# First attention: scaling-and-transposing products on two row halves, 64 queries each, into two banks

## The reference, cut to what matters

```
s = einsum("bqhpd,bkhpd->bhpqk", q, k) * (HEAD_DIM ** -0.5)
p = softmax(s, axis=-1)
a = p[:, :, 0] - lam * p[:, :, 1]
o = einsum("bhqk,bkhe->bqhe", a, v)
```

## Time and profile before

| | |
|---|---|
| median of three runs | 1553.6 us (1548.66 to 1557.16) |
| profiled execution | 1554.42 us |
| its span | 1552.6 us, mean granted TensorE clock 0.988 |
| TensorE multiplying, loading | busy 96%, 89% |
| VectorE, ScalarE | busy 73%, 49% |
| first attention's loops on TensorE | 169.6 to 246.5 us |
| transposing records (L969) | 256, busy 34.4 us |

### The profile page before, as it was taken

The page is one execution under the profiler, slowest core; times in us unless marked ns, Lnnn a source line. Parts: engine busy times, 40 slices in busy tenths (PEclk is TensorE's granted clock), DMA queues, the critical chain, the costliest instruction groups (busy, mean ns, idle before and its releaser), DMA issues.

```text
span 1552.6 us, 27950 instructions
## 1 busy us (share of the span) xinstructions
PE 1495.9 (96%) x11704; PEld 1384.9 (89%) x11704; DVE 1132.0 (73%) x1572; ACT 765.0 (49%) x911; POOL 11.5 (1%) x25
## 2 busy tenths in 40 slices
PE   7999999999999999999999999999999999999887
PEld 3999778999998886899999999988999999998786
DVE  6877785878887977655667566676587666878886
ACT  2422354566334441566434446544454334668784
POOL 0000000000000000000001000000000000000000
PEclk9999999999999999999999999999999999999999
DMA  9454434477775430245666454322354455778993
GB/s 370 154 204 148 152 111 165 149 281 271 292 279 214 178 136 27 109 175 194 227 236 245 167 186 160 141 104 110 140 199 159 164 195 190 299 291 323 361 370 117
DMA packets 43525, 310.27 MB, mean 200 GB/s; under 512 B 5239, under 2 KB 5624, under 8 KB 7000
## 3 DMA queue, kind: packets, MB, share of 16 engines
q1 hardware_dynamic: 41760, 301.75, 52.1%
q0 software_dynamic: 1264, 5.82, 1.1%
q10 hardware_dynamic: 392, 1.12, 0.2%
HBM read 307.63 MB, written 1.05 MB: 199 GB/s over the span
## 4 chain that ended last, share of the span: by engine, by line
PE 82%; DVE 9%; DMA 4%; ACT 3%; issue 1%; SPq 0%; DVEq 0%; ACTq 0%
PE ps L754 16%; PE ps L755 15%; PE ps L759 15%; DVE wlo L2240 3%; PE ps L969 2%; DMA raw<-weights_in 2%; PE ps L790 2%; PE ps L785 2%; PE ps L786 2%; ACT whi L1687 2%; PE ps L807 1%; DMA mstart<-mod_start_in 1%; PE ps L808 1%; PE ps L809 1%; PE ps L727 1%; PE ps L729 1%
## 5 line engine op out<-in xcount | busy, mean ns | idle before, releaser
L2240 DVE TENSOR_TENSOR wlo<-raw,whi 128x2048 fp32r<-128x2048 f32 x172 | 392.6, 2288 | 167.6 <-ACT whi L1687 166.8
L1687 ACT ACTIVATE whi<-raw 128x2048 fp32r<-128x2048 f32 x187 | 357.3, 1915 | 202.1 <-PE ps L759 114.7
L754 PE MATMUL ps<-uhi,whi 128*128 128x256 f32 x1232 | 294.4, 281 | 0.8 <-DVE y L2865 0.8
L755 PE MATMUL ps<-uhi,wlo 128*128 128x256 f32 x1232 | 288.4, 277 | 0.0
L754 PEld LDWEIGHTS ps<-uhi,whi 128*128 128x128 f32 x1232 | 231.4, 188 | 7.7 <-issue 6.3
L755 PEld LDWEIGHTS ps<-uhi,wlo 128*128 128x128 f32 x1232 | 231.3, 188 | 1.3 <-issue 1.2
L759 PE MATMUL ps<-ulo,whi 128*128 128x256 f32 x1232 | 164.9, 276 | 0.0
L759 PEld LDWEIGHTS ps<-ulo,whi 128*128 128x128 f32 x1232 | 151.3, 188 | 0.0
L754 PE MATMUL ps<-hid_hi,whi 128*128 128x256 f32 x512 | 122.1, 281 | 0.0
L755 PE MATMUL ps<-hid_hi,wlo 128*128 128x256 f32 x512 | 120.8, 278 | 0.0
L2259 DVE SCALAR_TENSOR_TENSOR macc<-raw,csil,macc 128x256 f32<-128x256 f32 x224 | 108.6, 485 | 7.8
(11 more groups left out here) (611 smaller groups left out, 3214.2 us busy)
## 6 DMA issues: line engine op xcount, KB each, us to landing
raw<-weights_in SPq DMA_DIRECT2D x225, 1024.0 KB, 4.8
raw_more<-weights_in SPq DMA_DIRECT2D x22, 1024.0 KB, 4.9
y<-weights_in SPq DMA_DIRECT2D x15, 1024.0 KB, 6.6
spare<-weights_in SPq DMA_DIRECT2D x14, 1024.0 KB, 6.6
mstart<-mod_start_in SPq DMA_DIRECT2D x4, 2048.0 KB, 18.8
w1c<-cmp_w_in POOLq DMA_DIRECT2D x1, 2048.0 KB, 13.6
h<-x_in SPq DMA_DIRECT2D x1, 1024.0 KB, 7.8
ctx<-ctx_in SPq DMA_DIRECT2D x1, 1024.0 KB, 30.1
```

The lines of the kernel that those rows point to most:

```text
L754: mm(o, wk(whi, k), x0[:, k0 + k, :], start=first and k == 0, stop=False)
L755: mm(o, wk(wlo, k), x0[:, k0 + k, :], start=False, stop=False)
L1687: fn(hi_at(i) if n is None else whi[:, sl, :], raw_at(i) if n is None else raw[:, sl, :], ACT.Copy).then_inc(s("hi_ready"), 1)
L2240: tt(lo_at(i), raw_at(i), f32(hi_at(i)), ALU.subtract).then_inc(s("lo_ready"), 1)
```

## The change

Each product of a block with the diagonal becomes two: the queries 0 to 63 (rows 0 to 63 of `ebuf`, the upper left quarter of `diag`) and the queries 64 to 127 (rows and columns 64 to 127). The two have 64 contraction rows each, stream 64 columns each, and write to two banks, 4 for the first half of the queries and 5 for the second. Off these quarters the diagonal matrix is zero, so nothing is lost. A unit now fills half of both banks, and the next unit uses the same places: TensorE waits for the copy of the unit just before (`att_copied` at u, not u - 1), from unit 1 on. ScalarE copies in two parts of 128x256, and it makes the copy of unit u - 2 ahead of `exps(u)`.

```
             def turn_weights(u):
                 pe.wait_ge(s("att_ready"), u + 1)
-                if u >= 2:
-                    pe.wait_ge(s("att_copied"), u - 1)
+                if u:
+                    pe.wait_ge(s("att_copied"), u)
                 for k in range(4):
                     for p in range(2):
-                        ins = mm(ps[:, 4 + u % 2, k * P:(k + 1) * P], ebuf[:, u % 2, p, k * P:(k + 1) * P], diag[:, u % 2, p, :],
-                                 start=p == 0, stop=p == 1)
+                        for half in range(2):
+                            a = slice(half * HD, (half + 1) * HD)
+                            ins = mm(ps[:, 4 + half, k * HD:(k + 1) * HD], ebuf[a, u % 2, p, k * P:(k + 1) * P], diag[a, u % 2, p, a],
+                                     start=p == 0, stop=p == 1)
                 ins.then_inc(s("att_turned"), 1)
...
             for u in range(2 * HEADS + 4):
-                if u < 2 * HEADS:
-                    exps(u)
                 if 2 <= u <= 2 * HEADS + 1:
                     v = u - 2
                     act.wait_ge(s("att_turned"), v + 1)
                     if v >= 4:
                         act.wait_ge(s("o_ready"), v // 2 - 1)
-                    fn(atb[:, (v // 2) % 2, :, (v % 2) * P:(v % 2 + 1) * P], ps[:, 4 + v % 2, :].rearrange("p (k q) -> p k q", k=4),
-                       ACT.Copy).then_inc(s("att_copied"), 1)
+                    for half in range(2):
+                        q0 = (v % 2) * P + half * HD
+                        ins = fn(atb[:, (v // 2) % 2, :, q0:q0 + HD], ps[:, 4 + half, 0:T].rearrange("p (k q) -> p k q", k=4), ACT.Copy)
+                    ins.then_inc(s("att_copied"), 1)
+                if u < 2 * HEADS:
+                    exps(u)
```

## The result

The changed kernel took 1554.62 us (12 runs, 1550.98 to 1567.6), the kernel before 1550.2 (12 runs). The ratio is 1.004, interval 1.0021 to 1.006: slower by 3 to 9 us, around the 0.5% that I had called no change for three runs, but not the +0.5 us of the sum. The mean granted clock of the changed kernel's runs is 0.9864. The profiled executions hide the difference: span 1552.5 after, 1552.6 before. The one before, 1554.42, was among the slower of its kernel (the 12 runs: 1544.98 to 1557.16). So the base of the sum, 1553.6, stood 3.4 us above the 1550.2, the move was put 4 us too low against the medians, and the predicted 1554.1 met the 1554.62 by luck of that base.

The account below looks back on a forecast made before the run. TensorE's own sequence was taken to bound the kernel, 82% of the last chain. Products 0, switches -0.6 and -0.3, end +1.4 gave +0.5 us: 1554.9 against the profiled execution, 1554.1 against the median, range 1548 to 1561.

Parts of the forecast that it names:

- the sum: Whole kernel: products 0, switches -0.6 and -0.3, end +1.4, together +0.5 us on the profiled 1554.42.
- Products: Turning units on TensorE: 128-column loads set the step, halves load together, 16 pairs at 0.112, 1.79 us; no change.
- A: Rival, turning units: the stream sets the step, each unit 0.86 us less, 13.8 in all, 1540.3; chance 4%.
- B: Rival, turning units: halves do not load wide weights together, +1.79 us a unit, +28.6, 1582.7; chance 4%.
- Switches: Row-mode changes around TensorE's units: -0.05 us each for units 2 to 13, -0.6, and -0.3 at the start.
- -0.3 of the first two units: Row-mode changes at the start, half clock: unit 1 loses 0.28 and 0.2 us, unit 0 gains 0.2.
- The wait: TensorE waiting for the previous unit's copy: hidden except between units 14 and 15, where it idles 1.09 us.
- +1.4: Attention's end, units 14 and 15: 1.09 us of idle TensorE plus 0.35 for row-mode changes.
- ScalarE's later exponentials: ScalarE copying first moves exponentials back by some 0.6 us; no cost taken, 1 us if a copy slips.
- C: Rival, turns with modulation: the copy comes late, 0.86 us on 7 units, +6, 1560; chance 3%.
- The clock: TensorE's granted clock in the first attention: expected at 1.00 from 185 us on, no cost in the sum.
- rival D: First attention: half-filled products keep the granted clock low, pieces at most double, +57 us, 1611; chance 2%.

Follow-up runs that it names:

- 128 columns streamed: Changed kernel with each half product streaming all 128 diagonal columns, 64 of them zero, instead of 64; ratio 1.0012 to the kernel before, 1551.49 us.
- quarters: Changed kernel with each half product cut again by keys, weights 64 columns wide, 64 records a unit; ratio 0.9979 to the kernel before, 1546.51 us.
- 128 columns and head squares: Changed kernel streaming all 128 diagonal columns, with the first six head-square sums moved between units 14 and 15; ratio 1.0004 to the kernel before, 1551.18 us.
- idle products ahead: Changed kernel with extra unused TensorE products, two behind the second scores and three behind the third; ratio 1.0029 to the kernel before, 1553.96 us.
- head squares between: Changed kernel with the first six head-square sums moved from behind unit 15 to between units 14 and 15; ratio 1.0028 to the kernel before, 1553.08 us.
- at the start with idle products: Kernel before with only extra unused TensorE products added, two behind the second scores and three behind the third; ratio 0.9994, 1550.34 us.

## Why the prediction was right or wrong

**Products, right.** The step is set by the load of 128 columns and both halves load at once: 16 pairs a unit, 1.73 in the chain. Halving the stream saved nothing (128 columns streamed: 1.78), halving the weights' columns did (quarters: 1.16). Rivals A and B fall. The 0.071 of L1253, a mean over two orders, could not decide this; the units do. The Trainium skill's rule in "TensorE: Matmul & The Clock Gate", LDWEIGHTS (a load goes by its columns, not by its rows), agrees with these three numbers in their order, though 1.16 is more than half of 1.73; the up to 2x of its "TensorEngine Tiling (Array Packing)", Theoretical Speedup, came for the quarters, which narrow the weights' columns as well, in part (1.16 against 1.73), and for the halves not at all.

**Switches, right.** 0.11 us per pair of turns, 0.05 a unit, came back, as summed. The -0.3 of the first two units cannot be read off, since they ran at another clock.

**The wait, right in place and size.** One idle stretch, ended by the copy. The wait alone cost +1.0 in the profile of the kernel before; in that of the kernel with 128 columns, from unit 14's start to the values behind the head squares, it is 7.58 us (233.82 to 241.40) against 6.25 before (234.38 to 240.63), +1.3 with the switches, where I had put +1.4. ScalarE's later exponentials held nobody up; C did not come.

**The clock, wrong.** The step that failed is rival D, in what I set against it: "records follow without gaps as before". They do, loads and all, and the clock still fell. I had given D 2%, and only at the price of the whole attention at 1.2 GHz, which did not come either; a part of it did. All my other chances, 98%, had gone to a clock that stays. The size: over the runs the clock is 0.9863 against 0.9903, and 0.0040 of some 1550 us is 6.2 us of TensorE at full speed; the means of those runs are 1556.59 and 1550.70, 5.9 apart. Among the 35 runs of the kernel before in that comparison 0.001 of clock goes with 1.3 us, and by this rate the 0.0040 is 5.4. For the kernel before with 64 columns it is 0.0057, 8.8 us or 7.6 by that rate, against 7.3 between the means. So most of the loss is the clock, with the wait's 1.0 beside it, within the noise of twelve runs (0.001 of clock). The cut of the stream is its cause: the same loads, waits, records and row halves with twice the columns had the clock of before, and the kernel before with half the columns lost it. The quarters, which send each half's columns through twice, once per half of the keys, kept the clock as far as can be told; they also take less time, and which of the two counts was not tested.

Open in part stays where in an execution the clock is lost. A profile shows one execution, and the stretch at the start varies whatever is streamed: in the profile of the kernel with 128 columns and head squares the clock had a mean of 0.57 over 174 to 186 us, though its runs have the clock of before. The table rests on the means over runs, not on one profile. That the fall at 238 us needs both the half stream and the wait fits the profiles: it stands in all three with both (the changed kernel twice, and with idle products ahead), and in none with only one of them (128 columns streamed, new wait in the kernel before, head squares between). But that is one execution each.

## What to carry to other kernels

Before narrowing a product, find out whether the load or the stream sets its step, from a place where only one of them is narrow; with fresh weights each time, cut the stationary operand's columns, not the stream. And ask of a change that takes streamed columns away what it does to the granted clock behind the next gap. Compare mean clocks over many runs, since one profile of each kernel may show the same span for two kernels that differ. But read from the chain what the clock is worth: where VectorE ends the turns, as at the start with idle products, a higher clock brought no time that could be told (0.9922 and a ratio of 0.9994).

## What the runs showed of the hardware that was not expected

- TensorE, busy without a gap from 185 to 200 us and with the same loads, was granted 1.2 GHz for those 15 us when each transposing record streamed 64 columns of 128 rows; with 128 columns the same list of products had 2.4 GHz there (one profile each; over the runs 0.9846 against 0.9903).
- Products on the four quarters of the array run beside each other: 64 records with their loads in 1.16 us, 18 ns each, where records with weights as wide on two alternating halves step at 29 ns.
- A change between whole-row and row-half work cost 0.2 us here (modulation 0.34 and 0.54, values 1.73 and 1.92), and none showed between two kinds of row-half work: scores to units, 1.06 then 1.73 with nothing between.
